# ScalarE makes one more high part before it empties a bank, in two projection loops and the expert queries

## What is computed

```python
u = rmsnorm_2(h, norm_mix_w)                 # 272 tokens x 1024
proj = u @ w_in                              # 1024 x 5136
z, xbc, dt_raw, conf_in = split(proj)        # 1024, 2048, 16, 2048 wide
xbc = silu(causal_depthwise_conv(xbc, conv_w, conv_b))     # 4 taps
dt = softplus(dt_raw + dt_bias)              # then the chunked state-space mixer
a, g = split(conf_in)
h2 = causal_depthwise_conv(a * sigmoid(g), conf_w, conf_b) # 31 taps
...                                          # mixer, layer norm, w_out, residual
q = rmsnorm_2(h, norm_ffn_w) @ w_query       # 8 heads x 256: the expert queries
s1, s2 = q1 @ sub_keys_1, q2 @ sub_keys_2    # scores; top 16 of each, then the experts
```

## Time and profile before

| | us |
|---|---|
| median of 3 runs | 1483.83 (1483.47 to 1485.14) |
| the profiled execution, its own time | 1479.37 |
| its span, first to last instruction | 1477.3 |
| PE busy in the span | 1412.1 (96%) |
| DVE busy | 1062.6 (72%) |
| ACT busy | 734.1 (50%) |
| mean granted TensorE clock | 0.982 |

### The profile page before, as it was taken

One profiled execution on the slowest core, in us unless ns is written; L12 is line 12 of the kernel. 1 busy time (PEld: TensorE's weight loads), 2 busy tenths in 40 slices (PEclk: granted clock), 3 DMA queues, 4 the chain that ended last, 5 costly groups with the idle time before them and its releaser, 6 DMA issues.

```text
span 1477.3 us, 25207 instructions
## 1 busy us (share of the span) xinstructions
PE 1412.1 (96%) x10482; PEld 1289.3 (87%) x10482; DVE 1062.6 (72%) x1721; ACT 734.1 (50%) x1052; POOL 2.5 (0%) x8
## 2 busy tenths in 40 slices
PE   6989799998899998899999999999999999999997
PEld 5877699997899986799999999999987777888886
DVE  4555666546699976777899987788878888655554
ACT  4554655545467736557444445434344444444443
POOL 0000000000000000000000000000000000000000
PEclk9999899999999899999999999999999999999999
DMA  6332255664455201255566555554555555556653
GB/s 240 115 100 86 76 195 185 189 198 132 153 171 158 86 1 43 72 184 176 157 190 184 187 181 185 163 167 162 168 160 169 171 164 167 183 185 200 188 188 108
DMA packets 63617, 228.59 MB, mean 155 GB/s; under 512 B 7312, under 2 KB 8208, under 8 KB 63376
## 3 DMA queue, kind: packets, MB, share of 16 engines
q1 hardware_dynamic: 61776, 223.90, 48.2%
q10 hardware_dynamic: 1728, 3.09, 0.6%
HBM read 225.91 MB, written 1.05 MB: 154 GB/s over the span
## 4 chain that ended last, share of the span: by engine, by line
PE 91%; DVE 6%; ACT 2%; issue 1%; DMA 1%; ACTq 0%; DVEq 0%
PE ps L291 18%; PE ps L292 17%; PE ps L293 17%; PE ps L850 8%; PE ps L851 8%; PE ps L852 8%; PE ps L595 2%; PE ps L816 2%; DVE W L1336 1%; DVE RSI L1342 1%; PE ps L478 1%; PE ps L341 1%; DMA plain<-in_masks 1%; DVE plain L1558 1%; PE ps L299 1%
## 5 line engine op out<-in xcount | busy, mean ns | idle before, releaser
L1336 DVE TENSOR_TENSOR W<-raw,W 128x1024 fp32r<-128x1024 f32 x423 | 515.3, 1221 | 289.2 <-ACT W L896 287.8
L896 ACT ACTIVATE W<-raw 128x1024 fp32r<-128x1024 f32 x423 | 446.5, 1057 | 383.5 <-PE ps L852 208.1
L291 PE MATMUL ps<-XH,W 128*128 128x256 f32 (+1 forms) x1592 | 453.4, 285 | 9.3 <-DVE W L1336 5.2
L292 PE MATMUL ps<-XL,W 128*128 128x256 f32 (+1 forms) x1592 | 450.1, 283 | 0.0
L293 PE MATMUL ps<-XH,W 128*128 128x256 f32 (+1 forms) x1592 | 448.0, 281 | 0.0
L291 PEld LDWEIGHTS ps<-XH,W 128*128 128x128 f32 x1592 | 298.7, 188 | 11.5 <-issue 7.0
L293 PEld LDWEIGHTS ps<-XH,W 128*128 128x128 f32 x1592 | 300.9, 189 | 0.0
L292 PEld LDWEIGHTS ps<-XL,W 128*128 128x128 f32 x1592 | 299.5, 188 | 0.0
L850 PE MATMUL ps<-W,HH 128*128 128x512 f32 x512 | 205.6, 402 | 0.8 <-ACT hid L1301 0.8
L851 PE MATMUL ps<-W,HH 128*128 128x512 f32 x512 | 202.8, 396 | 0.0
L852 PE MATMUL ps<-W,HL 128*128 128x512 f32 x512 | 202.8, 396 | 0.0
(11 more groups left out here) (311 smaller groups left out, 1949.9 us busy)
## 6 DMA issues: line engine op xcount, KB each, us to landing
raw<-in_w_dn SPq DMA_DIRECT2D x128, 512.0 KB, 3.5
raw<-in_w_up SPq DMA_DIRECT2D x128, 512.0 KB, 3.5
raw<-in_w_ff SPq DMA_DIRECT2D x64, 512.0 KB, 4.3
raw<-in_w_in SPq DMA_DIRECT2D x57, 512.0 KB, 3.6
raw<-in_w_out SPq DMA_DIRECT2D x24, 512.0 KB, 3.5
raw<-in_w_q SPq DMA_DIRECT2D x16, 512.0 KB, 3.8
raw<-in_w_kv SPq DMA_DIRECT2D x4, 512.0 KB, 3.4
plain1a<-in_memT ACTq DMA_DIRECT2D x1, 1024.0 KB, 11.3
```

The source lines that it names most:

```text
L291: e.matmul(out, wh, xh, start=first, stop=False, skip_group_check=shared)
L292: e.matmul(out, wh, xl, start=False, stop=False, skip_group_check=shared)
L896: e.activation(W[:, u % NSLOT, 0, :], raw[:, u % NRAW, :], ACT.Copy).then_inc(s["hi"], 1)
L1336: e.tensor_tensor(W[:, u % NSLOT, 1, :], raw[:, u % NRAW, :], W[:, u % NSLOT, 0, :], ALU.subtract).then_inc(s["lo"], 1)
```

## The change

It adds two calls of `hi_to` and raises the argument of a third, all in `scalar_program`. In GLU at even m and in WQ at odd m, the high part of unit m + 3 is made ahead of the wait for unit m and of the copy behind it. In XB this is done at every m. No other engine's program is touched.

```diff
                 hi_to(U_GLU + m + 3)
                 j = m // 2
                 if m % 2 == 0:
+                    hi_to(U_GLU + m + 4)
                     e.wait_ge(s["unit"], U_GLU + m + 1)
                     if j >= 2:
                         e.wait_ge(s["gp"], j - 1)
...
             for m in range(16):
-                hi_to(U_XB + m + 3)
+                hi_to(U_XB + m + 4)
                 e.wait_ge(s["unit"], U_XB + m + 1)
                 e.activation(XB[:, m, 3:275], ps[in2_bank(m)][:, 0:272], ACT.Copy).then_inc(s["xb"], 1)
...
                 if m % 2:
                     g = m // 2
+                    hi_to(U_WQ + m + 4)
                     e.wait_ge(s["unit"], U_WQ + m + 1)
                     if g >= 3:
                         e.wait_ge(s["q_l"], g - 2)
```

## The result

The changed kernel takes 1488.92 us (median of 7 runs, 1486.41 to 1491.08) against 1483.83 for the kernel before (7 runs, 1483.13 to 1485.14). The ratio is 1.0033, interval 1.0021 to 1.0045: **0.33% slower**, where 0.25% was forecast (1487.6, +3.8 us; measured +5.1).

What follows compares the result with a forecast made beforehand. TensorE was taken to bound the kernel, with VectorE full in XB and a loop through ScalarE just under its pace. 3.15 us up to L614 plus 0.62 in WQ gave 3.77, so 1483.83 became 1487.6; range 1484.6 to 1489.8.

Steps and rivals of the forecast that it cites:

- GLU 0: In GLU, Sigmoid comes 0.95 us later, but VectorE needs it only 3.00 us on: cost 0.
- XB, first pair 0.95, then 0.81 for every second pair, 2.57 in all: In XB, the delayed copy makes the six taps late, the delay builds up, and TensorE leaves 2.57 us later.
- once only: In XB the loop doesn't build up and costs 0.95 us; 2.1 us in all, 1485.9; chance 0.17.
- nothing: In XB, ScalarE has 12 us idle and catches up before anyone asks: 1483.8; chance 0.07.
- Rival faster: In XB, TensorE's six late starts are for want of a high part and go: 2.4 us gained, 1481.4; chance 0.05.
- Behind XB, the last Exp 0.95 later still, 0.58 more before L614: Behind XB, unit 15's copy has another high part ahead; ScalarE is 3.52 us late, L614 starts 3.15 us late.
- WQ 0.62: At the end of WQ, QL comes 0.95 us later and the low part behind it makes TensorE 0.62 us late.
- a fall of the clock in XB alone: Wider gaps in XB let TensorE's clock fall, costing 5.8 us more: 1493.4; chance 0.05.
- 12.52 against 12.66 us: In XB before, for two pairs: the way through TensorE and ScalarE back to the taps, against VectorE's own time.

Runs made afterwards that it cites:

- Experiment 2: Two kernels against before: XB's early high part, at odd m behind the first taps (1.0010); no high part moved, XB's copy delayed by three diagonals (1.0021).
- wq_only: Only the WQ line of the change, on the kernel before: 1485.29 us, ratio 1.0005.
- after_taps20: The changed kernel with 20 instead of 14 of TensorE's convolution taps ahead of L614 and 6 instead of 12 behind: 1481.70 us, ratio 0.9992 against before.
- both: The kernel before with 20 instead of 14 TensorE taps ahead of L614, and one instead of two VectorE taps at odd m in XB: 1477.60 us, ratio 0.9960.
- before_again: The kernel before, unchanged, profiled once more: 1484.91 us, ratio 1.0002.

## Why the prediction was right

- **GLU 0**: right; 0.9999 by itself, TensorE busy in all of 45 us. The table load for Sigmoid did move behind a high part, and nobody waited for it.
- **XB, first pair 0.95, then 0.81 for every second pair, 2.57 in all**: right in mechanism and size. Measured 49.65 - 46.98 = 2.67. From the first tap group to the last are 46.90 us (453.26 to 500.16), the sum gave 46.74. Experiment 2 shows that the copy's delay alone makes it, and that the same high part one place later costs nothing there.
- **Rivals once only and nothing**: fallen. The Trainium skill's rule ("Perfetto Trace Analysis", Identifying the Most-Contended Engine) would have had ScalarE, the emptiest of the three in XB, cost nothing; the runs show 0.24% from 0.95 us at each unit on it.
- **Rival faster**: fallen. Late starts were for want of VectorE's time: fewer taps on it removed them, earlier high parts didn't.
- **Behind XB, the last Exp 0.95 later still, 0.58 more before L614**: L608 to L614 grew by 0.60 to 0.69. Right; taking out the tail gave 1.01 back. That is more than 0.60 because the long first spell of the two profiles of before (10 us) had itself held up L608's end and VectorE's sum behind it: with a first spell of 7 us, wq_only has 16.43, and 17.43 is 1.00 above it.
- **WQ 0.62**: 0.60.
- These make 2.67 + 0.6 to 0.7 + 0.60 = 3.9 to 4.0 us, and the forecast had 3.77. Measured were 5.1. **The term that was mis-sized** is "behind XB": I took TensorE's 0.20 us of idle time at L614 as a sign that the delay passes straight through, put the stretch behind L614 at 0, and priced a fall of the clock in XB alone, as a rival at 0.05. In XB it held at 1.00. It fell behind L614, where TensorE now idled 2.55 us: 3.1 us in the profile. The 1.1 us that the median is above the sum is less than that, and a late spell by chance comes to an untouched stage too, as wq_only's profile shows. How often it comes in runs of either kernel isn't known, so the split of this 1.1 us between clock and spread isn't settled; that it costs 3.1 us in the profile of the changed kernel, and that after_taps20 is without it, is shown.
- **Luck**: the forecast had no term for this spell. Had every run of the changed kernel its 3.1 us and no run of before any, the difference would be 7.0 us, above the measured interval (3.1 to 6.7 us) and above the range of the forecast. That the time came out inside it means that the spell comes in some runs only, or comes to before as well, or is made up for elsewhere; nothing in the sum foresaw any of these.
- The size of TensorE's idle time itself came out larger than the delay, 2.55 instead of 0.2 + 0.6. The rest is the first slow spell: 7 us long in this profile and 10 in those of before, so TensorE was through its 14 taps 14.88 us behind L608 instead of 16.54, and waited instead.

## What to carry to other kernels

Work put ahead of a wait costs nothing only as long as nobody waits for what stands behind it: before moving an instruction up, add up the loop that leads from the delayed one back to itself (here 12.52 against 12.66 us, a slack of 0.14) and not the engine's share of busy time. A short, steady wait may be the visible end of a loop with almost no slack, and then each turn pays. And where an engine with much work to do is about to wait a few us, give it some of that work first: on the changed kernel that was worth 0.41%, more than the change cost.

## What the runs showed of the hardware

- The granted clock fell behind quite short idle times of TensorE. The idle time before L614 and the length of the stage behind it, in 14 profiles: none (twice), 0.20, 0.29, 0.31, 0.58 and 0.83 us of idle time with the clock at 1.00 behind it; 1.51, 1.54, 1.82, 2.51, 2.52 and 2.55 us, and 3.17, each with a spell at 1.2 GHz that made the stage 1.7 to 3.1 us longer. The idle time doesn't set the length: 2.52 us came with 1.7, 2.55 with 3.1. The Trainium skill ("TensorE: Matmul & The Clock Gate", The HAM clock gate) describes a default at half rate that activity releases; the rows agree as far as they show idle time ahead of each of these late falls; the first falls, next, had none.
- TensorE also fell to 1.2 GHz without any idle time, during or right behind the 48 small matmuls (16 columns) behind XB: for 7 to 10 us in most profiles, and for 3.5 us in the kernel "both" (a mean of 0.89 from 490 to 506), where the clock was 1.00 until the small matmuls ended at 495.8 and fell in the taps behind them. What that spell costs depends on whether TensorE, or who waits for it, had time to spare.
- Two profiles of one and the same kernel, before and before_again, differ by 5.6 us in span (1477.3 and 1482.9). 2.4 us of it arise before 97 us, at a clock of 0.97 against 0.93 in the first 100 us, and 1.8 and 1.5 us in the two later stretches named above. A span of one profile is no measure for a change of 0.3%. Marks within a stage are better, where the clock is the same in both: XB and L614 to L653 agreed to 0.1 us in these two, the stretch from YCH to RH didn't.
